# A transformer block on one core: the two small products of the forgetting-attention scores stacked in one contraction

## The chip, the cores and the metric

The kernel runs on one core of one Trainium2 chip. The metric is the device time of one execution in microseconds; the number quoted is the median of the runs. TensorE (PE) multiplies matrices, VectorE (DVE), ScalarE (ACT) and GpSimd (POOL) work on tiles of 128 partitions, SyncE (SP) and ACT start DMA transfers. Each engine runs its own list of instructions strictly in order, and waits on semaphores for the others.

## The reference, cut to what matters

Two transformer blocks over 1024 tokens of width 1024. The first block mixes pooling, gated linear attention and "Fox" attention with 8 heads of 64 channels, then an MLP; the second has multi-head latent attention ("MLA", 16 heads). Everything is float32. The change touches the Fox scores alone:

```
qh = heads(q) * (Dh ** -0.5)                       # 8 heads, Dh = 64
F  = cumsum(log_sigmoid(f_logit + b_f))
s  = einsum('bhqd,bhkd->bhqk', qb, kh) + Fb[..., None] - F[:, :, None, :]
s  = where(kpos <= qpos, s, -inf)
o  = softmax(s) @ v
```

## The kernel before, in words

**Precision.** A float32 operand is split in a "hi" part, rounded to the format that TensorE multiplies in one pass, and a "lo" part, the rest. A product is the sum of three: lo by hi, hi by lo, and hi by hi. This holds for the weight products (function `project`, line 220, 48 matmuls of 512 columns for a unit of 128 output channels) and for the scores.

**Fox buffers.** For each head there are four tiles of 128 partitions by 1024 tokens, each in two copies `b` = 0, 1 that alternate from head to head: `q_hi`, `q_lo`, `k_hi`, `k_lo`. Rows 0 to 63 hold the head's channels (line 967 by ACT; lines 983, 984, 987 by DVE). Row 64 of `k_hi` and `k_lo` holds the two parts of the forget sums, fetched by two row DMAs that ACT issues (line 963); row 65 of `q_hi` receives minus the row maximum by another row DMA (line 733). The constant rows are set once by POOL (line 1000). The contraction has 66 rows for scores and 65 for the row maxima.

**The step.** `steps` (line 843 and before) runs one step for each of the 8 heads: steps 0 and 1 written out, then a loop of two steps per turn. Step n projects the queries and keys of head n and finds its row maxima, and in the same step the scores, exponentials and value products of head n-1 are computed. TensorE's order in a step (`step_pe`, `attend_pe`):

- first half of the projection (24 matmuls), then scores 0 and 1 of head n-1, then the second half;
- twelve iterations g = 0 to 11 of `attend_pe`. The scores are cut in 12 pieces of at most 128 keys by 512 queries; their widths are 512, 384, 256, 256 (first half of the queries) and 512 five times, 384, 256, 256 (second half), six of 512, two of 384 and four of 256 in all. Iteration g has the value products of piece g (lines 622, 623: they wait for ACT's first exponential, line 668), the third value product of piece g-1 (line 629: waits for POOL, line 677), and the scores of piece g+2 (lines 606, 607, 608, and a mask matmul, 612, on the diagonal). After iterations 4 to 9 come the row maxima of head n (lines 652, 654, 655): maxima 0 and 1 after g = 4, 2 and 3 after g = 5, then one after each. Maxima 4 to 7 take PSUM banks again that DVE must have reduced: maximum 6 waits until maximum 4 is reduced;
- transposes of the values (638, 640), and of the eight maxima (660), which waits for DVE's line 717.

ACT computes two exponentials of each piece (668 to `p_hi`, 670 to `probs`), and between them what `fox_prepare_act` puts at certain g: the scaled copy of the queries at g = 1 (967), the copy of the values at g = 3 (973). After g = 6 it starts the softmax division of the first half (685, 687). POOL subtracts for each piece (677), then splits the weights of the next unit (1919, 1921). DVE splits queries and keys, reduces the maxima (712), and between maxima 3 and 4 does the division of the first half (698, 701, 707).

The last head has no step that projects another: `last_pe` and `last_act` attend to it alone.

## Time and profile before

| | |
|---|---|
| runs | 2280.11, 2282.21, 2282.62 us, median 2282.21 |
| profiled execution, span from first to last instruction | 2284.0 us |
| PE busy | 2128.9 us, 93% of the span |
| POOL, DVE, ACT busy | 1105.4, 1125.8, 671.8 us |
| mean granted TensorE clock | 0.964 of full speed |

The profiled execution has no time of its own beside its span, 2284.0 us, which lies 1.8 us above the median of the runs. The Fox stage is a small part: the steps of heads 1 to 7 run from 118.9 to 345.2 us of the span, the last head to 368.9 us. A row of the timeline gives the start and the length of an instruction (or of several alike that follow one another) and, in square brackets, how long the engine sat idle before it and what ended that. Matmuls overlap: the recorded length of one (0.40 us for 512 columns) is longer than the distance from its start to the next start, which is what it costs.

### The profile page before, as it was taken

What the parts mean: (1) busy time and instruction counts of PE and PEld (TensorE: products, weight loads), DVE (VectorE), ACT (ScalarE), POOL (GpSimd) and SP (SyncE); (2) the same over time, 40 slices, a digit from 0 to 9 for tenths busy, and PEclk for the clock granted to TensorE, in tenths of its full rate; (3) what the DMA queues carried; (4) which work ended last, traced back from release to release, by engine and by line L of the source; (5) the groups of instructions that cost most, each with busy time, mean ns of one, the idle gap of its engine ahead of it and who ended that gap; (6) DMA issues with size and microseconds to landing.
All of it is one profiled execution on the core that took longest, in us unless ns stands there. A gap on an engine that the chain in (4) does not pass through costs nothing.

```text
span 2284.0 us, 27160 instructions
## 1 busy us (share of the span) xinstructions
PE 2128.9 (93%) x9840; PEld 1691.4 (74%) x9840; DVE 1125.8 (49%) x1213; ACT 671.8 (29%) x1069; POOL 1105.4 (48%) x657
## 2 busy tenths in 40 slices
PE   5999999988999999999999998998999999989996
PEld 3777776877778878788878876886776777668774
DVE  6545653737541211212111287215777777754576
ACT  3334444221121000000001132114555555560322
POOL 1635554522833634633444383334656666653373
PEclk9999998997999999999999998998999999989998
DMA  3100000112211211211111131110000000001122
GB/s 139 48 19 20 14 14 19 46 38 92 92 46 53 67 55 46 74 46 54 57 55 46 55 101 37 46 46 28 20 19 19 19 19 19 19 28 46 46 69 97
DMA packets 31624, 106.98 MB, mean 47 GB/s; under 512 B 3440, under 2 KB 3632, under 8 KB 31568
## 3 DMA queue, kind: packets, MB, share of 16 engines
q1 hardware_dynamic: 27520, 96.53, 12.7%
q10 hardware_dynamic: 4048, 9.67, 1.2%
q8 instruction: 39, 0.64, 0.1%
q14 instruction: 17, 0.14, 0.0%
HBM read 101.83 MB, written 4.26 MB: 46 GB/s over the span
## 4 chain that ended last, share of the span: by engine, by line
PE 59%; POOL 15%; issue 14%; DVE 8%; ACT 2%; ACTq 0%; POOLq 0%; DMA 0%; DVEq 0%
PE ps L220 45%; POOL probs_lo L677 11%; PE ps L385 4%; PE ps L249 3%; PE ps L237 2%; POOL w_lo L1921 2%; POOL w_hi L1919 2%; DVE h_lo L366 1%; DVE tmp L1747 1%; DVE x L1749 1%; DVE S_all L1287 1%; DVE tmp L362 1%; DVE result L1753 0%; PE ps L1594 0%; DVE ssq L413 0%
## 5 line engine op out<-in xcount | busy, mean ns | idle before, releaser
L1919 POOL TENSOR_TENSOR w_hi<-w_raw,zero 128x1024 fp32r<-128x1024 f32 (+1 forms) x173 | 334.7, 1935 | 816.0 <-PE ps L220 575.7
L1921 POOL TENSOR_TENSOR w_lo<-w_raw,w_hi 128x1024 fp32r<-128x1024 f32 (+1 forms) x173 | 433.0, 2503 | 13.6
L220 PE MATMUL ps<-h_hi,w_lo 128*128 128x512 f32 x1328 | 338.4, 398 | 5.6 <-DVE x L512 5.1
L220 PE MATMUL ps<-h_hi,w_hi 128*128 128x512 f32 x1328 | 328.0, 389 | 0.0
L677 POOL TENSOR_TENSOR probs_lo<-probs,mla_p_hi 128x512 fp32r<-128x512 f32 x192 | 220.3, 1167 | 182.0 <-ACT probs L670 181.9
L220 PE MATMUL ps<-h_lo,w_hi 128*128 128x512 f32 x1216 | 302.0, 391 | 0.0
L220 PEld LDWEIGHTS ps<-h_hi,w_lo 128*128 128x128 f32 x1328 | 251.2, 191 | 61.6 <-issue 10.0
L220 PEld LDWEIGHTS ps<-h_hi,w_hi 128*128 128x128 f32 x1328 | 249.3, 188 | 51.7
L220 PEld LDWEIGHTS ps<-h_lo,w_hi 128*128 128x128 f32 x1216 | 230.0, 189 | 48.4
L1369 DVE TENSOR_TENSOR tmp<-ps,tmp 128x1024 f32<-128x1024 f32 x22 | 26.9, 1224 | 370.3 <-PE ps L220 363.6
L712 DVE TENSOR_REDUCE mx<-ps 128x1 f32<-128x256 f32 (+1 forms) x192 | 144.5, 785 | 78.5 <-PE ps L655 77.8
L677 POOL TENSOR_TENSOR probs_lo<-probs,fox_p_hi 128x512 fp32r<-128x512 f32 (+1 forms) x96 | 102.9, 1081 | 126.8 <-ACT probs L670 126.1
L670 ACT ACTIVATE probs<-ps 128x512 f32<-128x512 f32 (+2 forms) x288 | 145.7, 506 | 0.0
L512 DVE TENSOR_TENSOR x<-ps,x 128x1024 f32 x32 | 39.1, 1222 | 171.7 <-PE ps L220 165.1
L668 ACT ACTIVATE mla_p_hi<-ps 128x512 fp32r<-128x512 f32 x192 | 97.6, 508 | 85.2 <-PE ps L612 55.6
L1357 ACT ACTIVATE tmp<-ps 128x1024 f32<-128x1024 f32 x22 | 22.6, 1027 | 323.4 <-PE ps L220 323.3
L1359 ACT ACTIVATE a_hi<-tmp 128x1024 f32 x22 | 23.4, 1062 | 236.8 <-DVE tmp L1369 236.8
L622 PE MATMUL ps<-mla_p_hi,mla_vaug 128*128 128x512 f32 x192 | 79.4, 413 | 8.5 <-ACT mla_p_hi L668 6.8
L668 ACT ACTIVATE fox_p_hi<-ps 128x512 fp32r<-128x512 f32 (+1 forms) x96 | 48.5, 505 | 100.8 <-PE ps L612 94.3
L1371 DVE TENSOR_TENSOR a_lo<-tmp,a_hi 128x1024 f32 x22 | 59.8, 2718 | 29.4 <-ACT a_hi L1359 29.4
L629 PE MATMUL ps<-probs_lo,mla_vaug 128*128 128x512 f32 x192 | 68.7, 358 | 4.4 <-POOL probs_lo L677 4.4
L606 PE MATMUL ps<-mla_q_hi,mla_k_lo 97*128 97x512 f32 x192 | 69.1, 360 | 3.3 <-DMA mla_q_hi<-c_neg 3.3
(345 smaller groups left out, 3911.7 us busy)
## 6 DMA issues: line engine op xcount, KB each, us to landing
w_raw<-in_wpack SPq DMA_DIRECT2D x173, 512.0 KB, 3.3
x<-in_xT ACTq DMA_DIRECT2D x16, 512.0 KB, 8.3
out<-result SPq DMA_DIRECT2D x8, 512.0 KB, 2.9
p_raw<-in_pT ACTq DMA_DIRECT2D x1, 1024.0 KB, 7.2
const_stage<-in_consts SPq DMA_DIRECT2D x1, 788.0 KB, 4.4
pos_i<-in_pos SPq DMA_DIRECT2D x1, 512.0 KB, 6.4
vec<-in_vecs SPq DMA_DIRECT2D x1, 284.0 KB, 5.3
mla_q_hi<-c_neg ACTq DMA_DIRECT2D x16, 4.0 KB
```

What stands on the lines that cost most here:

```text
L220: last = nc.tensor.matmul(dst[:, half, :], w[slot][:, kt, :], a[:, i, t], start=(n == 0), stop=(n == total - 1))
L249: last = nc.tensor.matmul(dst[:, half, :], w[u % 2][:, kt, :], a[:, kt, cols(half)], start=(kt == 0 and n == 0), stop=(kt == DT - 1 and n ...
L385: last = nc.tensor.matmul(PS[:, bank, :], w[slot][:, kt, :], a[:, kt, t], start=(k == 0), stop=(k == 3 * len(order) - 1))
L606: nc.tensor.matmul(out, k_lo[b][r, keys], q_hi[b][r, t], start=True, stop=False)
L622: nc.tensor.matmul(PS[:, O_BANK[half], off:HALF], A.bufs[4][b][:, j, :], p, start=(j == 0), stop=False)
L629: nc.tensor.matmul(PS[:, O_BANK[half], off:HALF], A.bufs[4][b][:, j, :], P_lo[g % 4][:, 0:HALF - off], start=False, stop=(g in LAST_OF_HAL ...
L668: nc.scalar.activation(A.p_hi[g % 2][:, 0:HALF - off], scores, ACT.Exp).then_inc(A.p_hi_done, 1)
L670: nc.scalar.activation(Pt[g % 4][:, 0:HALF - off], scores, ACT.Exp).then_inc(A.exp_done, 1)
L677: nc.gpsimd.tensor_tensor(P_lo[g % 4][:, w], Pt[g % 4][:, w], A.p_hi[g % 2][:, w].bitcast(F32), ALU.subtract)\
L712: nc.vector.reduce_max(mx[:, i:i + 1], flat(PS[:, bank:bank + 2, :])[:, 0:max_width(i)[1]] if i >= 4 else PS[:, bank, 0:max_width(i)[1]], ...
L1919: nc.gpsimd.tensor_tensor(w_hi[s][:, kts, :], raw[s][:, kts, :], no_change[:, kts, :], ALU.add).then_inc(w_hi_done, 1)
L1921: nc.gpsimd.tensor_tensor(w_lo[s][:, kts, :], raw[s][:, kts, :], w_hi[s][:, kts, :].bitcast(F32), ALU.subtract)\
```

## The change

In the Fox attention `k_lo` and `q_lo` become stacks of 128 rows: `q_lo` holds the hi queries in rows 0 to 63 and the lo queries in rows 64 to 127, `k_lo` the lo keys in rows 0 to 63 and the hi keys in rows 64 to 127. One matmul over all 128 rows gives both small products. The hi by hi product still needs hi queries and hi keys on the same rows, so ACT copies both into `q_hi` and `k_hi` (two more copies of 64 by 1024). The two parts of the forget sums sit in rows 64 and 65 of `k_hi`, filled by one DMA of two rows; the row maximum moves to row 66. POOL sets 6 tiles at the start instead of 10. MLA keeps its three products.

```diff
-            nc.tensor.matmul(out, k_lo[b][r, keys], q_hi[b][r, t], start=True, stop=False)
-            nc.tensor.matmul(out, k_hi[b][r, keys], q_lo[b][r, t], start=False, stop=False)
+            if A is fox:
+                nc.tensor.matmul(out, k_lo[b][:, keys], q_lo[b][:, t], start=True, stop=False)
+            else:
+                nc.tensor.matmul(out, k_lo[b][r, keys], q_hi[b][r, t], start=True, stop=False)
+                nc.tensor.matmul(out, k_hi[b][r, keys], q_lo[b][r, t], start=False, stop=False)
             last = nc.tensor.matmul(out, k_hi[b][r, keys], q_hi[b][r, t], start=False, stop=not masked)
...
-        fox = Attention("fox", FOX_H, HD + 1, HD + 2, 0)
+        fox = Attention("fox", FOX_H, HD + 2, HD + 3, 0)
...
                     if A is fox:
-                        pe.wait_ge(A.f_in[b], turn * 32 + 32)
+                        pe.wait_ge(A.copied, (n + 1) * 2)
+                        pe.wait_ge(A.f_in[b], turn * 16 + 16)
...
-            for part, row in ((0, k_hi[b]), (1, k_lo[b])):
-                act.dma_start(row[HD:HD + 1, :].bitcast(F32), f_rows[part, bass.ds(n, 1), :]).then_inc(fox.f_in[b], 16)
+            act.dma_start(k_hi[b][HD:HD + 2, :].bitcast(F32), f_rows[:, bass.ds(n, 1), :].rearrange("a o t -> (a o) t")).then_inc(fox.f_in[b], 16)
...
-                nc.scalar.activation(q_hi[b][0:HD, :], src[0:HD, :], ACT.Copy, scale=HD ** -0.5).then_inc(fox.hi_done, 1)
+                nc.scalar.activation(q_lo[b][0:HD, :], src[0:HD, :], ACT.Copy, scale=HD ** -0.5).then_inc(fox.hi_done, 1)
+
+            def queries_again():
+                act.wait_ge(fox.hi_done, n * 2 + 1)
+                nc.scalar.activation(q_hi[b][0:HD, :], q_lo[b][0:HD, :].bitcast(F32), ACT.Copy).then_inc(fox.copied, 1)
+
+            def keys_again():
+                act.wait_ge(fox.hi_done, n * 2 + 2)
+                nc.scalar.activation(k_hi[b][0:HD, :], k_lo[b][HD:P, :].bitcast(F32), ACT.Copy).then_inc(fox.copied, 1)
...
-            return {1: queries, 3: values}
+            return {1: queries, 2: queries_again, 3: keys_again, 4: values}
...
-            nc.vector.tensor_copy(k_hi[b][0:HD, :], src[HD:P, :]).then_inc(fox.hi_done, 1)
-            nc.vector.scalar_tensor_tensor(q_lo[b][0:HD, :], src[0:HD, :], HD ** -0.5, q_hi[b][0:HD, :].bitcast(F32),
+            nc.vector.tensor_copy(k_lo[b][HD:P, :], src[HD:P, :]).then_inc(fox.hi_done, 1)
+            nc.vector.scalar_tensor_tensor(q_lo[b][HD:P, :], src[0:HD, :], HD ** -0.5, q_lo[b][0:HD, :].bitcast(F32),
                                            ALU.mult, ALU.subtract).then_inc(fox.lo_done, 1)
             dve.wait_ge(fox.hi_done, n * 2 + 2)
-            nc.vector.tensor_tensor(k_lo[b][0:HD, :], src[HD:P, :], k_hi[b][0:HD, :].bitcast(F32), ALU.subtract)\
+            nc.vector.tensor_tensor(k_lo[b][0:HD, :], src[HD:P, :], k_lo[b][HD:P, :].bitcast(F32), ALU.subtract)\
                 .then_inc(fox.lo_done, 1)
...
-                for dst, value in ((q_hi[b][HD:HD + 2, :], 1.0), (q_lo[b][HD:HD + 2, :], 0.0), (k_hi[b][HD:HD + 2, :], 1.0),
-                                   (k_lo[b][HD:HD + 2, :], 0.0), (vaug[b][:, :, HD:P], 1.0)):
-                    nc.gpsimd.memset(dst.bitcast(F32), value).then_inc(fox.setup, 1)
+                for dst in (q_hi[b][HD:HD + 3, :], k_hi[b][HD:HD + 3, :], vaug[b][:, :, HD:P]):
+                    nc.gpsimd.memset(dst.bitcast(F32), 1.0).then_inc(fox.setup, 1)
```

ACT's list in a step, from the scaled copy of the queries at g = 1 to the first exponential of piece 5; `fox_p_hi` and `probs` are written by the two exponentials of pieces 2, 3, 4 and 5 in turn. Before:

```order
L967 ACTIVATE fox_q_hi_92<-ps 64x1024
L668 ACTIVATE fox_p_hi_103<-ps 128x256
L670 ACTIVATE probs_81<-ps 128x256
L668 ACTIVATE fox_p_hi_104<-ps 128x256
L670 ACTIVATE probs_82<-ps 128x256
L973 ACTIVATE fox_vT<-mix 64x1024
L668 ACTIVATE fox_p_hi_103<-ps 128x512
L670 ACTIVATE probs_79<-ps 128x512
L668 ACTIVATE fox_p_hi_104<-ps 128x512
```

The same stretch of ACT's list in the changed kernel:

```order
L971 ACTIVATE fox_q_lo_94<-ps 64x1024
L671 ACTIVATE fox_p_hi_103<-ps 128x256
L673 ACTIVATE probs_81<-ps 128x256
L975 ACTIVATE fox_q_hi_92<-fox_q_lo_94 64x1024
L671 ACTIVATE fox_p_hi_104<-ps 128x256
L673 ACTIVATE probs_82<-ps 128x256
L979 ACTIVATE fox_k_hi_96<-fox_k_lo_98 64x1024
L671 ACTIVATE fox_p_hi_103<-ps 128x512
L673 ACTIVATE probs_79<-ps 128x512
L985 ACTIVATE fox_vT<-mix 64x1024
L671 ACTIVATE fox_p_hi_104<-ps 128x512
```

A copy stands ahead of the exponentials of piece 3, another ahead of those of piece 4, and the values' copy has moved from ahead of piece 4 to ahead of piece 5.

TensorE's list in iterations g = 3 and g = 4: value products, scores of pieces 5 and 6, and the first maximum. Before:

```order
L622 MATMUL ps<-fox_p_hi_104,fox_vaug_99 128x256
L623 MATMUL ps<-fox_p_hi_104,fox_v_lo_101 64x256
L629 MATMUL ps<-probs_lo_85,fox_vaug_99 128x256
L606 MATMUL ps<-fox_q_hi_91,fox_k_lo_97 128x512
L607 MATMUL ps<-fox_q_lo_93,fox_k_hi_95 128x512
L608 MATMUL ps<-fox_q_hi_91,fox_k_hi_95 128x512
L622 MATMUL ps<-fox_p_hi_103,fox_vaug_99 128x512
L623 MATMUL ps<-fox_p_hi_103,fox_v_lo_101 64x512
L629 MATMUL ps<-probs_lo_86,fox_vaug_99 128x256
L606 MATMUL ps<-fox_q_hi_91,fox_k_lo_97 128x512
L607 MATMUL ps<-fox_q_lo_93,fox_k_hi_95 128x512
L608 MATMUL ps<-fox_q_hi_91,fox_k_hi_95 128x512
```

The same two iterations in the changed kernel:

```order
L625 MATMUL ps<-fox_p_hi_104,fox_vaug_99 128x256
L626 MATMUL ps<-fox_p_hi_104,fox_v_lo_101 64x256
L632 MATMUL ps<-probs_lo_85,fox_vaug_99 128x256
L607 MATMUL ps<-fox_q_lo_93,fox_k_lo_97 128x512
L611 MATMUL ps<-fox_q_hi_91,fox_k_hi_95 128x512
L625 MATMUL ps<-fox_p_hi_103,fox_vaug_99 128x512
L626 MATMUL ps<-fox_p_hi_103,fox_v_lo_101 64x512
L632 MATMUL ps<-probs_lo_86,fox_vaug_99 128x256
L607 MATMUL ps<-fox_q_lo_93,fox_k_lo_97 128x512
L611 MATMUL ps<-fox_q_hi_91,fox_k_hi_95 128x512
```

One matmul of each piece's three score products is gone; nothing else has moved on this engine.

## Rows read from the trace of the kernel before

**Rows 1.** Stretches: us; busy of PE, PEld, DVE, ACT, POOL; PEclk; DMA share, GB/s.

```profile
148.00:156.00 8.00, 7.09 (x33) 5.39 (x32) 6.32 (x8) 1.72 (x4) 4.95 (x3) 0.79 0.14 42
181.00:190.00 9.00, 8.10 (x45) 6.44 (x44) 6.42 (x9) 1.88 (x4) 4.97 (x3) 1.00 0.16 61
151.50:184.60 33.10, 31.99 (x160) 24.55 (x159) 17.61 (x22) 14.82 (x30) 16.97 (x15) 0.95 0.05 17
1745.00:1755.00 10.00, 8.36 (x53) 6.25 (x53) 9.14 (x10) 4.69 (x11) 8.03 (x7) 1.00 0.00 0
```

**Rows 2.** Timeline (start, length in us), TensorE: scores 0, then projection.

```profile
158.70 0.40 PE L606 MATMUL ps<-fox_q_hi,fox_k_lo 66*128 66x512 f32 x1
158.93 0.40 PE L607 MATMUL ps<-fox_q_lo,fox_k_hi 66*128 66x512 f32 x1
...
162.02 1.98 PE L220 MATMUL ps<-h_lo,w_hi 128*128 128x512 f32 x8
```

**Rows 3.** Timeline, ACT: the same step, iterations 1 to 5.

```profile
165.84 1.02 ACT L967 ACTIVATE fox_q_hi<-ps 64x1024 fp32r<-64x1024 f32 x1 [4.33 <-PE ps L220]
...
166.76 0.37 ACT L668 ACTIVATE fox_p_hi<-ps 128x256 fp32r<-128x256 f32 x1
...
167.03 0.37 ACT L670 ACTIVATE probs<-ps 128x256 f32<-128x256 f32 x1
...
167.86 0.38 ACT L668 ACTIVATE fox_p_hi<-ps 128x256 fp32r<-128x256 f32 x1 [0.46 <-PE ps L612]
...
168.40 1.05 ACT L973 ACTIVATE fox_vT<-mix 64x1024 f32 x1
...
169.35 0.58 ACT L668 ACTIVATE fox_p_hi<-ps 128x512 fp32r<-128x512 f32 x1
...
170.30 0.59 ACT L668 ACTIVATE fox_p_hi<-ps 128x512 fp32r<-128x512 f32 x1
```

**Rows 4.** Timeline, TensorE: value products 3, 4, 5; mask and maximum 6.

```profile
168.76 0.28 PE L622 MATMUL ps<-fox_p_hi,fox_vaug 128*128 128x256 f32 x1
...
170.07 0.47 PE L622 MATMUL ps<-fox_p_hi,fox_vaug 128*128 128x512 f32 x1
...
171.84 0.48 PE L622 MATMUL ps<-fox_p_hi,fox_vaug 128*128 128x512 f32 x1
...
178.85 0.23 PE L612 MATMUL ps<-masks,ident_bf 128*128 128x128 bf16 x1
...
179.19 0.50 PE L652 MATMUL ps<-fox_k_hi,fox_q_hi 65*128 65x512 f32 x1
```

**Rows 5.** Timeline, DVE and POOL: division of the first half.

```profile
174.95 0.69 DVE L698 TENSOR_TENSOR newton<-ps,r 64x512 f32<-64x512 f32 x1
...
175.44 3.95 POOL L677 TENSOR_TENSOR probs_lo<-probs,fox_p_hi 128x512 fp32r<-128x512 f32 x3 [1.11 <-ACT probs L670]
...
175.68 1.60 DVE L701 SCALAR_TENSOR_TENSOR rec<-newton,r 64x512 f32<-64x512 f32 x1
...
177.46 0.68 DVE L707 SCALAR_TENSOR_TENSOR mix<-ps,rec 64x512 f32 x1 [0.18 <-DVE rec L701]
```

**Rows 6.** Timeline, end of the step: POOL, DVE, TensorE.

```profile
182.51 1.89 POOL L1919 TENSOR_TENSOR w_hi<-w_raw,zero 128x1024 fp32r<-128x1024 f32 x1
...
182.88 1.55 DVE L717 TENSOR_SCALAR mx<-mx 128x8 f32<-128x8 f32 x1
...
184.49 0.27 PE L660 MATMUL ps<-ident,mx 128*8 128x128 f32 x1 [0.69 <-DVE mx L717]
```

**Rows 7.** Timeline, TensorE: first score of the last head.

```profile
348.51 0.80 PE L606 MATMUL ps<-fox_q_hi,fox_k_lo 66*128 66x512 f32 x1 [3.28 <-DMA fox_q_hi<-c_neg]
```

**Rows 8.** Timeline, TensorE: a stall in the MLA stage.

```profile
1749.38 0.50 PE L652 MATMUL ps<-mla_k_hi,mla_q_hi 96*128 96x512 f32 x1 [0.74 <-DVE mx L712]
```

**Rows 9.** Timeline, step 0: ACT's queries, TensorE's first maximum.

```profile
103.27 1.02 ACT L967 ACTIVATE fox_q_hi<-ps 64x1024 fp32r<-64x1024 f32 x1 [12.85 <-POOL fox_vaug L1000]
...
108.33 0.28 PE L654 MATMUL ps<-fox_k_hi,fox_q_hi 65*128 65x256 f32 x1
```

More of the change, by code:

```diff
@@ L733, in max_row_act @@
             act.dma_start(A.bufs[0][b][A.rows - 1:A.rows, :].bitcast(F32), c_neg[:, :].bitcast(F32)).then_inc(A.row_in[b], 16)
-        fox = Attention("fox", FOX_H, HD + 1, HD + 2, 0)
+        fox = Attention("fox", FOX_H, HD + 2, HD + 3, 0)
         fox.bufs, fox.v_lo, fox.p_hi = buffers("fox", R_X, R_X + 24576, R_S + 8192, R_S + 20480, R_S + 24576)
         fox.f_in = [sem(f"fox_f_in{b}") for b in range(2)]
+        fox.copied = sem("fox_copied")
         fox_vT = at("fox_vT", R_S + 16384, [HD, T])
@@ L957, in fox_prepare_act @@
             if isinstance(n, int) and n == 0:
-                act.wait_ge(fox.setup, 10)
+                act.wait_ge(fox.setup, 6)
                 act.wait_ge(f_stored, 32)
@@ L980, in fox_prepare_dve @@
             if isinstance(n, int) and n == 0:
-                dve.wait_ge(fox.setup, 10)
+                dve.wait_ge(fox.setup, 6)
             dve.wait_ge(fox.hi_done, n * 2 + 1)
-            nc.vector.tensor_copy(k_hi[b][0:HD, :], src[HD:P, :]).then_inc(fox.hi_done, 1)
-            nc.vector.scalar_tensor_tensor(q_lo[b][0:HD, :], src[0:HD, :], HD ** -0.5, q_hi[b][0:HD, :].bitcast(F32),
+            nc.vector.tensor_copy(k_lo[b][HD:P, :], src[HD:P, :]).then_inc(fox.hi_done, 1)
+            nc.vector.scalar_tensor_tensor(q_lo[b][HD:P, :], src[0:HD, :], HD ** -0.5, q_lo[b][0:HD, :].bitcast(F32),
                                            ALU.mult, ALU.subtract).then_inc(fox.lo_done, 1)
             dve.wait_ge(fox.hi_done, n * 2 + 2)
-            nc.vector.tensor_tensor(k_lo[b][0:HD, :], src[HD:P, :], k_hi[b][0:HD, :].bitcast(F32), ALU.subtract)\
+            nc.vector.tensor_tensor(k_lo[b][0:HD, :], src[HD:P, :], k_lo[b][HD:P, :].bitcast(F32), ALU.subtract)\
                 .then_inc(fox.lo_done, 1)
```

## The prediction

> **What bounds the kernel.** I read the page first: TensorE is busy 93% of 2284.0 us, every other engine under half. So the time is TensorE's list plus its stalls, and I went to the Fox stage by stretches. In the step that starts at 151.5 us TensorE is busy 31.99 of 33.10 us, with a mean clock of 0.95 [rows 1]; POOL has 16.97 us and ACT 14.82. The timeline of TensorE shows what one score matmul costs: of 512 columns, 0.23 us from start to start, though each is recorded as 0.40 [rows 2]. By columns I take 0.17 for 384 and 0.12 for 256. Then the other engines' timelines, to see which waits are close behind: ACT in the first five iterations, where the change puts work [rows 3, 4], DVE and POOL in the division between the maxima [rows 5], and the step's end [rows 6].
>
> **What is removed.** One score matmul in each of 12 pieces: 6 x 0.23 + 2 x 0.17 + 4 x 0.12 = 2.2 us for a head. If TensorE alone set the pace, 8 heads would give 17.8 us. The stacked matmul has 128 rows where the old ones had 66; the hi by hi one grows to 67, the maxima to 66. I cost the rows at nothing: eight of the projection's 128-row matmuls take 1.98 us, the last one's tail of 0.4 included, which is the same 0.23 each [rows 2].
>
> **What is added, and where it stands.** ACT gets two copies of 64x1024 in each step. The nearest row is the values' copy, SBUF to SBUF in the same shape: recorded 1.05 us, next instruction 0.95 after its start [rows 3]. The bounds are the queries' copy from PSUM (0.92 to the next) and no overlap at all (1.05). ACT has 18 us spare in the step, but not here: in iterations 2 to 5 the pieces are narrow and TensorE is right behind ACT. I walk the step on the clock of before, with value product 0 held at its place (165.65 us, just ahead of rows 3).
>
> - Scores 0 and 1 lie inside the projection, where nobody but TensorE counts: 0.23 + 0.17 = 0.40 us earlier for all that follows. I add it at the end.
> - Exponential 2 stands at 166.76 as before, its second at 167.03, the queries' new copy at 167.30. It puts piece 3 at 168.25 instead of 167.86. Piece 3 is done at 168.63, so value product 3 starts at about 168.75, where it stood at 168.76 [rows 4]: the 0.47 us that scores 2, 3 and 4 gave are spent waiting.
> - Piece 3's second at 168.52, the keys' copy at 168.79, piece 4 at 169.74 instead of 169.35. Value product 4 starts 0.72 after its exponential did, so at 170.46: +0.4, after about 0.9 us of idle TensorE.
> - Piece 4's second at 170.22, the values' copy (moved) at 170.70, piece 5 at 171.65 instead of 170.30. Value product 5 at 172.38: +0.55. This is the worst point.
> - From here ACT is ahead again, and each iteration is shorter by its score matmul: value product 6 at +0.3, 7 at +0.1, 8 at -0.1.
> - Maximum 6 waited for DVE: 0.34 us from the mask's start, where these follow a mask after 0.04 [rows 4], so 0.30 of stall. DVE was late because its line 701, which reads two SBUF operands, took 1.60 us where its neighbours of the same shape take 0.69 and 0.68: POOL had begun piece 7 at 175.44, DVE came at 175.68, and the two take turns [rows 5]. In the changed kernel ACT reaches piece 7 late: its chain (exponentials 5 and 6, two division steps) is some 0.7 us behind, so POOL begins it near 176.1 to 176.2, while DVE, tied to TensorE's maximum 3 (+0.3), comes at 176.0. DVE is now first by about 0.1 to 0.2 us, line 701 takes 0.7, and the stall of 0.30 goes.
> - So value product 9 is at -0.5, and 10 at -0.6. The end keeps its shape: POOL's last piece, then its weight split of 1.89 us, behind which line 717 waits for 1.55, then TensorE's 0.69 us of idle before line 660 [rows 6]. All of it follows the last scores, so -0.6.
>
> The Trainium skill, "SBUF — State Buffer", section "SBUF: two separate sides", says that VectorE with two SBUF inputs and GpSimd share a port pair as an exclusive lock: whoever starts first holds it for the whole instruction. The stretched 701 agrees with that. By the rule order at one moment decides 0.9 us of DVE, so it is also what could turn the last 0.3 around (first rival).
>
> Per step: 0.40 + 0.60 = 1.0 us earlier, seven steps: 7.0 us.
>
> **The last head.** It starts after 3.28 us of idle on the row DMA [rows 7], without ACT copies. TensorE sets the pace for pieces 0 to 5 (0.23 + 0.17 + 0.12 + 0.12 + 0.23 + 0.23 = 1.1 us saved, up to 1.8 where the clock is at its lower level); behind that ACT and POOL do. I take 1.1.
>
> **Edits at nothing.** Four memsets fewer on POOL release ACT's first queries some 4 us earlier; they waited 12.85 us for POOL [rows 9], but TensorE projects values until 108.33 before it needs a maximum, and that cover stays. The single row DMA saves one issue in ACT's queue, during the projection, where ACT waits for TensorE (4.33 us even right before the queries' copy [rows 3]). The new wait of TensorE for both copies comes before maximum 0, after value product 4, which itself needs ACT to be past the second copy: never late. Maximum 2 needs the values' copy, done at 171.75, ahead of value product 5. DVE's three operations keep shapes and sources.
>
> **Sum.** 7.0 + 1.1 = 8.1 us off the profiled 2284.0: 2275.9. The median of the runs is 1.8 us under that execution, so 2274.2; I say 2274.5.
>
> **Rivals.**
>
> 1. *POOL keeps the lead over line 701.* For it: the margin of 0.1 to 0.2 us is no more than my errors along the walk. Then 701 ends with POOL's piece 7 plus 0.5 us, near 177.9 instead of 177.28, maximum 6 comes at 179.8, the end of the step at +0.45, less 0.40: nothing gained in seven steps, 1.1 in the last head. 2281.5. Some steps one way, some the other: between.
> 2. *The clock falls in the new idle (the other side).* In the step's end before the stretch 148 to 156 the granted clock was 0.79, in 181 to 190 1.00 [rows 1]: every second step end costs 0.21 x 8 = 1.7 us, after a little more idle than its neighbour. The change makes new idle ahead of value products 3, 4 and 5: 0.5 + 0.9 + 0.4 = 1.8 us in 4. Should TensorE drop to the lower of its two levels (1.2 instead of 2.4 GHz) there, a step costs 1.7 more instead of 1.0 less; from five steps of seven on the kernel is slower than before. All seven: 7 x 1.7 - 8.1 = +3.8, so 2286.0; with rival 1 on top 2293. Against it: in the MLA stage TensorE stalls 0.74 us between dense matmuls [rows 8] with the clock at 1.00 over that stretch [rows 1]. The Trainium skill, "TensorE: Matmul & The Clock Gate", section "What's actually happening", calls the throttled state the default, which activity releases; the row at 0.79 agrees, and nothing here has as much idle amid dense work as the new place.
> 3. *The falls that are there disappear.* The step ends keep their shape, but all stands elsewhere in time. There are three such falls (at the ends of 151, 216 and 281 us; those of 184, 249 and 314 have none, one of each kind in [rows 1]). All three gone: 5 us more, 2269.5. For it: ends so much alike, with and without a fall. Against it: the same every second end keeps its extra idle.
> 4. *The copies are covered and all 17.8 us come.* 2264.4. It needs a copy of under 0.5 us; the row says 0.95.
>
> With the copies at 1.05 the walk loses 0.2 us per step, with 0.92 it gains 0.06: 2276 to 2274.
>
> **Chances.** Forecast 0.53, own range 2272 to 2278; rival 1, or a mixture, 0.24; rival 2 0.09; rival 3 0.10; rival 4 0.04. The range leaves out rival 4, most of rival 2 and the far end of 3: 2269.5 to 2283. Below 0.2% (4.6 us; the runs lie 2.5 us apart) a measurement tells nothing. Faster by more: nearly all of the forecast, rivals 3 and 4, a little of the mixtures, 0.62. Slower by more: rival 2 in most steps with rival 1, and what I overlook, 0.08. Same 0.30.
>
> **What would show it.** Per step, from one line 660 to the next: about 1.0 us less. TensorE waits for ACT ahead of value products 3, 4 and 5 (0.5, 0.9, 0.4 us). Line 701's successor, shorter than 0.8 us in the first half of each step, and no stall ahead of maximum 6: right; 1.6 us or more: rival 1. Granted clock under 1 between value products 4 and 7: rival 2. Total TensorE work less by 96 matmuls. I am wrong on the first term if the step ends are not at least 0.4 us earlier, and on the copies if value product 5 doesn't come later, measured from value product 0, than before.

## The result and the profile after

The changed kernel takes 2270.82 us (median of 4 runs, 2268.62 to 2272.18), the kernel before 2282.41 us (4 runs, 2280.11 to 2283.28): a ratio of 0.9944, 95% interval 0.9927 to 0.9961. A second series gave 2272.00 us against 2282.63, ratio 0.9953 (0.9939 to 0.9967). The forecast was 2274.5, the range 2269.5 to 2283.0. So the kernel is faster, by 11.6 and 10.6 us where 8 were forecast. The forecast's own range began at 2272; the point is nearer to rival 3 (2269.5), which adds 5 us from the clock to the forecast's 8.

Between the two profiled executions the span falls by 13.6 us, from 2284.0 to 2270.4. The step ends split that up. In the changed kernel line 663 is what line 660 was; from one such row to the next:

| | first end | steps of heads 1 to 7 (us) | last end to first matmul behind Fox | from there to the end |
|---|---|---|---|---|
| before | 118.84 | 32.40, 33.25, 31.44, 33.46, 31.46, 33.42, 30.68 | 34.83 | 1904.2 |
| after | 117.79 | 31.58, 30.66, 30.44, 30.97, 30.42, 30.91, 29.66 | 33.08 | 1904.9 |
| difference | -1.05 | -0.82, -2.59, -1.00, -2.49, -1.04, -2.51, -1.02 | -1.75 | +0.7 |

The seven steps give 11.5 us. The other columns move with the execution as well: a second profile of each kernel has its first end at 118.28 before and 118.52 after, so the 1.05 us of that column are no gain of the change; its last head takes 36.24 before and 33.07 after; and its seven steps add up to 226.2 and 214.6 us, 11.7 apart. Steps 3, 5 and 7 have full clock in both kernels, and give the forecast's 1.0 us each. Steps 2, 4 and 6 give 2.5 us: before, each began with the clock at its lower level [rows 1], and now none does. The page of the changed kernel has 96 matmuls fewer (9744), and a mean granted clock of 0.969 where it was 0.964.

The stretches of the changed kernel that answer to [rows 1]: the first end of the three in question, the next end, and one whole step (columns as there):

```profile
148.17:154.37 6.20, 5.51 (x30) 4.44 (x29) 4.72 (x7) 0.97 (x2) 3.51 (x2) 1.00 0.20 61
...
178.83:185.03 6.20, 5.50 (x31) 4.52 (x30) 4.72 (x7) 0.97 (x2) 3.51 (x2) 1.00 0.25 78
...
149.37:180.03 30.66, 28.51 (x146) 21.34 (x146) 16.90 (x22) 16.60 (x32) 17.05 (x15) 1.00 0.06 19
```

TensorE now sits idle for 2.15 us of the 30.66 where it was idle for 1.11 of 33.10: the change has turned part of the work it removed into waiting. ACT has grown from 14.82 to 16.60 us.

TensorE's timeline, changed kernel, scores 0 and 1 inside the projection; they answer to [rows 2]:

```profile
155.15 0.39 PE L607 MATMUL ps<-fox_q_lo,fox_k_lo 128*128 128x512 f32 x1
...
155.38 0.39 PE L611 MATMUL ps<-fox_q_hi,fox_k_hi 67*128 67x512 f32 x1
...
155.65 0.42 PE L607 MATMUL ps<-fox_q_lo,fox_k_lo 128*128 128x384 f32 x1
```

128 rows cost what 66 did: 0.23 us from the first start to the second. Score 1 starts 0.50 after score 0, where the old lines 606 stood 0.74 apart (158.70 and 159.44).

ACT in iterations 1 to 5 (start, length; in brackets the idle time before), for [rows 3]:

```profile
161.87 1.02 ACT L971 ACTIVATE fox_q_lo<-ps 64x1024 fp32r<-64x1024 f32 x1 [4.14 <-PE ps L220]
162.79 0.36 ACT L671 ACTIVATE fox_p_hi<-ps 128x256 fp32r<-128x256 f32 x1
163.05 0.37 ACT L673 ACTIVATE probs<-ps 128x256 f32<-128x256 f32 x1
163.32 1.05 ACT L975 ACTIVATE fox_q_hi<-fox_q_lo 64x1024 fp32r<-64x1024 f32 x1
164.27 0.37 ACT L671 ACTIVATE fox_p_hi<-ps 128x256 fp32r<-128x256 f32 x1
164.53 0.37 ACT L673 ACTIVATE probs<-ps 128x256 f32<-128x256 f32 x1
164.93 1.06 ACT L979 ACTIVATE fox_k_hi<-fox_k_lo 64x1024 fp32r<-64x1024 f32 x1
165.89 0.57 ACT L671 ACTIVATE fox_p_hi<-ps 128x512 fp32r<-128x512 f32 x1
166.37 0.58 ACT L673 ACTIVATE probs<-ps 128x512 f32<-128x512 f32 x1
166.97 1.06 ACT L985 ACTIVATE fox_vT<-mix 64x1024 f32 x1
167.94 0.57 ACT L671 ACTIVATE fox_p_hi<-ps 128x512 fp32r<-128x512 f32 x1
```

No row after the first has an idle time: ACT runs without a gap from 161.87, and is the engine that TensorE waits for. A copy takes 0.95 us to the next start, as the forecast took it.

TensorE in the same step, for [rows 4]: value products 3, 4 and 5, then the mask and maximum 6.

```profile
164.69 0.39 PE L625 MATMUL ps<-fox_p_hi,fox_vaug 128*128 128x256 f32 x1 [0.20 <-ACT fox_p_hi L671]
...
166.61 0.47 PE L625 MATMUL ps<-fox_p_hi,fox_vaug 128*128 128x512 f32 x1 [0.84 <-ACT fox_p_hi L671]
...
168.56 0.50 PE L625 MATMUL ps<-fox_p_hi,fox_vaug 128*128 128x512 f32 x1 [0.21 <-ACT fox_p_hi L671]
...
174.84 0.23 PE L615 MATMUL ps<-masks,ident_bf 128*128 128x128 bf16 x1
174.88 0.47 PE L655 MATMUL ps<-fox_k_hi,fox_q_hi 66*128 66x512 f32 x1
```

The three waits are where the forecast put them. Maximum 6 follows its mask after 0.04: its stall is gone.

DVE and POOL in the division, for [rows 5]:

```profile
172.19 0.69 DVE L704 SCALAR_TENSOR_TENSOR rec<-newton,r 64x512 f32<-64x512 f32 x1
...
172.43 4.49 POOL L680 TENSOR_TENSOR probs_lo<-probs,fox_p_hi 128x512 fp32r<-128x512 f32 x4 [0.82 <-ACT probs L673]
```

DVE's line 704 (the old 701) starts 0.24 us ahead of POOL's piece 7, and takes 0.69 instead of 1.60 us.

The step's end, for [rows 6], keeps its shape:

```profile
178.06 1.89 POOL L1930 TENSOR_TENSOR w_hi<-w_raw,zero 128x1024 fp32r<-128x1024 f32 x1
...
178.43 1.55 DVE L720 TENSOR_SCALAR mx<-mx 128x8 f32<-128x8 f32 x1
...
180.03 0.27 PE L663 MATMUL ps<-ident,mx 128*8 128x128 f32 x1 [0.70 <-DVE mx L720]
```

The first score of the last head, for [rows 7], still waits 3.28 us for the row DMA, 12.5 us earlier; and step 0, for [rows 9], shows ACT's queries 4.6 us earlier with TensorE's first maximum only 0.33 earlier:

```profile
98.63 1.02 ACT L971 ACTIVATE fox_q_lo<-ps 64x1024 fp32r<-64x1024 f32 x1 [8.53 <-POOL fox_vaug L1011]
...
108.00 0.28 PE L657 MATMUL ps<-fox_k_hi,fox_q_hi 66*128 66x256 f32 x1
...
335.99 0.80 PE L607 MATMUL ps<-fox_q_lo,fox_k_lo 128*128 128x512 f32 x1 [3.28 <-DMA fox_q_hi<-c_neg]
```

### The profile page after: what moved, and what is told of

Same layout as the page of the kernel before. It is cut to its first block, busy times and chain, and to the rows that moved or that the text cites. A ratio compares the mean times of both kernels' runs of the same rounds, so it can differ in the third digit from the quotient of the medians.

```text
span 2270.4 us, 26966 instructions
## 1 busy us (share of the span) xinstructions
PE 2106.5 (93%) x9744; PEld 1669.2 (74%) x9744; DVE 1118.9 (49%) x1213; ACT 685.6 (30%) x1085; POOL 1101.0 (48%) x653
## 4 chain that ended last, share of the span: by engine, by line
PE 58%; POOL 15%; issue 15%; DVE 9%; ACT 2%; ACTq 0%; POOLq 0%; DMA 0%; DVEq 0%
PE ps L220 45%; POOL probs_lo L680 11%; PE ps L385 4%; POOL w_lo L1932 2%; PE ps L237 2%; PE ps L249 2%; POOL w_hi L1930 2%; DVE h_lo L366 1%; DVE tmp L1758 1%; DVE x L1760 1%; DVE S_all L1298 1%; DVE tmp L362 1%; DVE ssq L1846 0%; DVE result L1764 0%; PE ps L1605 0%
## 5 line engine op out<-in xcount | busy, mean ns | idle before, releaser
L1932 POOL TENSOR_TENSOR w_lo<-w_raw,w_hi 128x1024 fp32r<-128x1024 f32 (+1 forms) x173 | 432.5, 2500 | 13.6
```

What stands on the lines that cost most here:

```text
L1932: nc.gpsimd.tensor_tensor(w_lo[s][:, kts, :], raw[s][:, kts, :], w_hi[s][:, kts, :].bitcast(F32), ALU.subtract)\
```

## The experiments

All were compared with the kernel before on the same chip. In the quoted expectations theory A is the account of the prediction: removed matmuls at their price, copies that hold TensorE up, the shared port, and falls of the clock apart from all that. What the other letters stand for is told in the texts themselves. The totals turned out a poor gauge for a single step: from the first matmul behind Fox to the end the same code takes 1898.6 to 1904.9 us from one profile to another, while the steps of the same kernel agree within 0.08 us (the first of them apart). So most verdicts below rest on the step lengths, and this table has them. A star marks a step, from the second on, that begins with a fall of the clock at the end before it (the first begins at the lower level in all of them).

| kernel | steps of heads 1 to 7 (us) |
|---|---|
| no_copies | 31.96, 31.10*, 31.15*, 29.83, 29.55, 29.79, 28.79 |
| copies_three_products | 32.74, 33.53*, 31.70, 33.64*, 32.09, 32.20, 31.34 |
| division_no_lock | 33.27, 31.25, 31.31, 33.11*, 31.29, 33.11*, 30.52 |
| values_first | 32.29, 31.64*, 30.00, 30.40, 31.58*, 30.38, 29.24 |
| keys_late_dve_copy | 31.25, 30.61, 30.23, 30.93, 30.24, 30.91, 29.47 |
| queries_early_keys_late | 30.61, 29.79, 29.67, 31.71*, 29.67, 31.66*, 30.45* |
| after_later | 32.16, 30.68, 30.44, 30.96, 30.43, 30.94, 29.67 |
| before_later_10 | 32.35, 33.19*, 31.43, 33.47*, 31.46, 33.46*, 30.69 |
| values_first_later | 31.15, 30.12, 30.00, 31.83*, 30.00, 30.38, 30.82* |

### no_copies: the matmul gone, without the copies

The kernel before, without one small product in Fox:

```diff
-            nc.tensor.matmul(out, k_hi[b][r, keys], q_lo[b][r, t], start=False, stop=False)
+            if A is not fox:
+                nc.tensor.matmul(out, k_hi[b][r, keys], q_lo[b][r, t], start=False, stop=False)
```

> The kernel before without the product of the hi keys with the lo queries (line 607) in all 12 Fox pieces of a head: TensorE's list as short as in the changed kernel, no second copies, the values' copy where it was. That product is left out of the scores. Theory A (my walk: the matmuls are worth 2.2 us a head, and ACT's copies eat the part of it between value products 2 and 5): steps of heads 1 to 7 shorter by 2.0 us each (0.40 in the projection, 1.6 behind it) against 1.0 in the changed kernel; no stall of 0.8 us ahead of value product 4; 2282.4 - 14 - 1.5 = 2267 with the three clock falls at the step ends still there, 2262 with them gone. Theory B (POOL and ACT would pace the step anyway, the copies cost little): steps shorter by no more than 1.2 us, 2270 to 2273.

Measured: 2262.83 us (4 runs), ratio 0.9909 (0.9892 to 0.9925). Steps 5 and 7, at full clock in both, are 1.91 and 1.89 us shorter than before. The removed matmul is worth 1.9 us of the 2.2 it costs, and against the changed kernel (0.87 less in steps 5 and 7, 1.14 and 1.12 in 4 and 6) the copies cost about 1.0 us in each step, as A has it. TensorE's waits between 118 and 335 us (us in total, times, longest), here and, in the second fence, in the changed kernel; line 623 here is 625 there, the value product:

```profile
PE ps L623 <- ACT fox_p_hi L669: 4.3, 7, 0.7
```

```profile
PE ps L625 <- ACT fox_p_hi L671: 8.0, 18, 0.8
```

Even without the new copies TensorE waits 4.3 us for ACT, once in each step, where it waited 0.7 us before the change: the shorter list of TensorE runs into the values' copy, which was there all along. That is 0.6 us a step. Part of it comes back at maximum 6: here too DVE reaches the line that was 701 ahead of POOL's piece 7 (172.72 against 172.94 us in step 2), and it takes 0.68 or 0.69 us in all seven steps. So the 1.9 us are the 2.2, less a new wait, plus an old stall that is gone; these parts add up to 1.7 or 1.8 in steps 5 and 7, and the rest was not followed. The new copies double the total of the waits.

### copies_three_products: the copies without the saving

The changed kernel, with the stacked matmul issued twice:

```diff
                 nc.tensor.matmul(out, k_lo[b][:, keys], q_lo[b][:, t], start=True, stop=False)
+                nc.tensor.matmul(out, k_lo[b][:, keys], q_lo[b][:, t], start=False, stop=False)
```

> The changed kernel with the stacked matmul issued twice (the small products are counted twice): ACT's list as in the changed kernel, TensorE's as long as before. Theory A: the copies alone cost: value product 4 at +0.4 and 5 at +0.6 us from value product 0, little of it made up, steps 0.3 to 0.4 us longer than before where neither has a clock fall, so +2.5 us: 2285 with falls, 2280 if they go. Theory B: copies are covered, steps as long as before within 0.1 us.

Measured: 2281.75 us (10 runs), ratio 0.9992 (0.9980 to 1.0004). All steps but the sixth are 0.18 to 0.66 us longer than before (steps 3, 5 and 7: 0.26, 0.63, 0.66), which is A's mechanism. The total isn't longer, and my number for it (2285) was a miss: step 6 lost its fall, and nothing in this run says why.

Steps 3 and 5 have the same instructions and full clock, and differ by 0.39 us (31.70 and 32.09). The trace shows where. The line that was 701 is 705 here; POOL's row is piece 7. In step 3, then in step 5:

```profile
207.08 0.68 DVE L705 SCALAR_TENSOR_TENSOR rec<-newton,r 64x512 f32<-64x512 f32 x1
207.08 1.83 POOL L681 TENSOR_TENSOR probs_lo<-probs,fox_p_hi 128x512 fp32r<-128x512 f32 x1 [0.81 <-ACT probs L674]
...
272.40 1.29 POOL L681 TENSOR_TENSOR probs_lo<-probs,fox_p_hi 128x512 fp32r<-128x512 f32 x1 [0.81 <-ACT probs L674]
272.41 1.82 DVE L705 SCALAR_TENSOR_TENSOR rec<-newton,r 64x512 f32<-64x512 f32 x1
...
276.00 0.50 PE L656 MATMUL ps<-fox_k_hi,fox_q_hi 66*128 66x512 f32 x1 [0.20 <-DVE mx L716]
```

The two reach their instructions within 0.01 us of each other. Where POOL is ahead, it takes its usual 1.29 us and DVE 1.82; where it is not, DVE takes 0.68 and POOL 1.83. In step 5 maximum 6 starts 0.43 us behind its mask (275.57), in step 3 0.04 behind (210.25 and 210.29): the same 0.39. Step 7 is like step 5, steps 1, 2, 3, 4 and 6 like step 3. This is rival 1, in two steps of seven and in the one kernel where the race is this close. It also says what the copies cost by themselves: 0.63 and 0.66 us against a kernel before whose 701 is just as long (steps 5 and 7), and 0.39 against `division_no_lock` below, where it is just as short (step 3). Beside the shorter list of TensorE the same copies cost 0.87 to 1.14 us a step: the halves of the change don't add, since a shorter list exposes more of the copies.

### division_no_lock: DVE's division without a second SBUF operand

The kernel before; in Fox, line 701 reads its second operand from PSUM:

```diff
-            nc.vector.scalar_tensor_tensor(rec[rows, :], newton[0:HD, :], -2.0, r0[0:HD, :], ALU.add, ALU.mult).then_inc(A.newton, 1)
+            second = PS[HD:P, O_BANK[half], :] if A is fox else r0[0:HD, :]
+            nc.vector.scalar_tensor_tensor(rec[rows, :], newton[0:HD, :], -2.0, second, ALU.add, ALU.mult).then_inc(A.newton, 1)
```

> The kernel before, with the second operand of line 701 taken from PSUM and not from SBUF in Fox (a wrong factor in the division). Theory A (the stall of 0.3 us ahead of maximum 6 comes from line 701 taking turns with POOL): line 701 takes 0.7 us and not 1.6, the stall goes, steps shorter by 0.3 us, 2282.4 - 2 = 2280.3. Theory B (the stall comes from the length of DVE's list, the port doesn't matter): 701 stays at 1.6 or the stall stays, no change.

Measured: 2280.58 us (10 runs), ratio 0.9990 (0.9979 to 1.0001); steps 3 to 7 are 0.13, 0.35, 0.17, 0.31 and 0.16 us shorter. DVE's division and TensorE's mask and maximum 6 in the step that starts at 151.30:

```profile
174.06 0.69 DVE L702 SCALAR_TENSOR_TENSOR rec<-newton,ps 64x512 f32<-64x512 f32 x1
```

```profile
177.22 0.23 PE L612 MATMUL ps<-masks,ident_bf 128*128 128x128 bf16 x1
177.26 0.48 PE L652 MATMUL ps<-fox_k_hi,fox_q_hi 65*128 65x512 f32 x1
```

0.69 us instead of 1.60, and no stall ahead of maximum 6. The link from the long 701 to the stall is shown. It is worth 0.31 and 0.35 us in steps 4 and 6, as the forecast had it, and 0.13 to 0.17 in steps 3, 5 and 7. That is because the forecast read the stall in an even step. In step 3 of the kernel before, maximum 6 starts 0.17 us behind its mask (210.45 and 210.62), a stall of 0.13.

### values_first: the copies away from the narrow pieces

The changed kernel, with the values' copy ahead of all and the two new ones behind pieces 3 and 4:

```diff
-            return {1: queries, 2: queries_again, 3: keys_again, 4: values}
+            if isinstance(n, int) and n == 0:
+                return {1: queries, 2: queries_again, 3: keys_again, 4: values}
+            return {0: values, 1: queries, 3: queries_again, 4: keys_again}
```

> The changed kernel with ACT's copies in another order from step 1 on: the values' copy ahead of the exponentials of piece 1, while ACT waits for the projection, then queries after piece 1, the second queries after piece 3, the second keys after piece 4. Theory A (what is left of the cost is where the copies stand): value products 3 and 4 no longer wait for a copy, 5 at about its old distance, steps shorter than in the changed kernel by 0.5 to 0.7 us, 2270.8 - 4.5 = 2266.3 without new clock falls. Theory B (the copies' place doesn't matter, since TensorE's wait moves to DVE or POOL): 2270 to 2272.

Measured: 2268.82 us (6 runs), ratio 0.9941 (0.9927 to 0.9954). The steps without a fall (3, 4, 6, 7) are 0.44, 0.57, 0.53 and 0.42 us shorter than the changed kernel's, two of them under the 0.5 to 0.7 that I gave. TensorE's waits between 118 and 335 us:

```profile
PE ps L625 <- ACT fox_p_hi L671: 4.3, 7, 0.7
...
PE ps L657 <- ACT fox_k_hi L979: 1.1, 3, 0.4
```

The waits for the exponentials fall from 8.0 to 4.3 us, and a little comes back at maximum 0, which needs the keys' copy. The total gains less than the steps: this kernel has two falls where the changed one has none.

### after_again, before_again, before_later: is a fall luck?

The changed kernel and the kernel before once more, and the kernel before with five matmuls more ahead of its Fox stage, whose result is overwritten; they were meant to move the stage by 1.1 us:

```diff
             pe.wait_ge(w_split, U_FV[1] + 3)
+            for _ in range(5):
+                nc.tensor.matmul(FV_BANKS[1][:, 0, :], w_hi[U_FV[1] % 2][:, 0, :], h_hi[:, 0, 0:HALF], start=True, stop=True)
             project(pe, U_FV[1] % 2, range(DT), h_hi, h_lo, FV_BANKS[1])
```

> The changed kernel once more, unchanged, for a second profile and a longer series. Theory C (the three clock falls at the ends of every second step, which were in the first profile of before and not in the first of after, come and go with where the step ends stand in time, from execution to execution, and are not removed by the change): the steps without a fall are again 30.4 to 31.0 us long, some ends may show a fall of 1.4 to 1.7 us now, and the median lies 2 to 4 us above the first series or the same, 2270 to 2275. Theory D (the change itself removes them, since TensorE's work about the step's end is different): no fall at any step end again.

> The kernel before once more, for a second profile. Theory C: another pattern of falls at the step ends is possible, and odd steps without one are 31.4 us again. Theory D: the same three ends (about 151, 216, 281 us) show a fall again.

> The kernel before with five more matmuls of 512 columns (1.1 us) in the values' projection ahead of the Fox steps (overwritten by the projection, so nothing else changes): all step ends later by 1.1 us. Theory C: the number of ends with a fall may differ from three; steps without a fall keep their length. Theory D: three falls as in before.

Measured: the changed kernel 2272.00 us (5 runs), its steps 31.49, 30.66, 30.41, 30.99, 30.41, 30.94, 29.68, no fall at the end of any step from 1 to 6. The kernel before, 2282.73 (one run): steps 32.55, 33.18, 31.46, 33.48, 31.45, 33.42, 30.70, falls at the step ends of 150.83, 215.47 and 280.40 us, which are those of steps 1, 3 and 5 again. With five matmuls more, 2283.23 (one run): falls at the same three ends, 151.30, 215.94 and 280.85. But its first end stands at 118.79 us, and at 118.84 and 118.28 in the two profiles without them: the five matmuls did not move the stage as they were meant to, and this run is one more profile of the kernel before. What the three show is that C in its first form is out: the falls aren't drawn anew in each profiled execution. They came at the same step ends although the whole stage stood up to 0.56 us apart.

### keys_late_dve_copy: one copy to DVE

Values first, the keys' copy at iteration 4, and the queries' second copy on DVE behind its three operations:

```diff
-            return {1: queries, 2: queries_again, 3: keys_again, 4: values}
+            if isinstance(n, int) and n == 0:
+                return {1: queries, 3: keys_again, 4: values}
+            return {0: values, 1: queries, 4: keys_again}
...
                 .then_inc(fox.lo_done, 1)
+            nc.vector.tensor_copy(q_hi[b][0:HD, :], q_lo[b][0:HD, :].bitcast(F32)).then_inc(fox.copied, 1)
```

> The version that the runs so far point to: values' copy first as in values_first, the second copy of the queries on DVE behind its three operations, the second copy of the keys on ACT after piece 4. Theory A: value products 3 and 4 wait for no copy and 5 hardly, what is left is a stall of some 0.5 us ahead of maximum 0, which needs both copies; steps shorter than in values_first by 0.2 to 0.5 us, 2268.8 - 2.5 = 2266.3. Theory B: DVE's copy (two sides in SBUF) collides with POOL and the maxima come later by as much: 2268 to 2270.

Measured: 2273.34 us (6 runs), ratio 0.9961 (0.9948 to 0.9974), 7 us over what I expected and 3 over theory B's 2270. The six runs lie far apart, 2264.9 to 2278.7, and the profile is of the fastest, so the steps speak for that one alone. Steps 2 to 7 are only 0.00 to 0.21 us shorter than the changed kernel's. TensorE's waits, 118 to 335 us:

```profile
PE ps L657 <- DVE fox_k_lo L997: 4.3, 4, 1.1
...
PE ps L657 <- DVE fox_q_hi L999: 3.6, 3, 1.2
```

DVE's end of its three operations, its copy, and TensorE's maximum 0 in one of these steps:

```profile
256.71 1.23 DVE L997 TENSOR_TENSOR fox_k_lo<-ps,fox_k_lo 64x1024 fp32r<-64x1024 f32 x1
257.97 0.82 DVE L999 CAST fox_q_hi<-fox_q_lo 64x1024 fp32r<-64x1024 f32 x1
```

```profile
258.89 0.36 PE L657 MATMUL ps<-fox_k_hi,fox_q_hi 66*128 66x256 f32 x1 [1.07 <-DVE fox_k_lo L997]
```

The wait for ACT is gone whole, and one of 1.1 us ahead of maximum 0 stands in its place: DVE is done with the copy at 258.79, TensorE starts at 258.89. (The trace names line 997, done at 257.94; it is the copy that came last.) I had counted DVE's free time in the step, and not when its result is due. Of theory B a part is there too: POOL begins piece 7 some 0.8 us ahead of line 704, which takes 1.00 to 1.07 us in all seven steps instead of 0.68.

### after_later, before_later_10, values_first_later: does the place in time decide?

Ten such matmuls ahead of the Fox stage, in the changed kernel, in the kernel before, and in values_first:

```diff
+            for _ in range(10):
+                nc.tensor.matmul(FV_BANKS[1][:, 0, :], w_hi[U_FV[1] % 2][:, 0, :], h_hi[:, 0, 0:HALF], start=True, stop=True)
```

> The changed kernel with ten more matmuls of 512 columns (2.3 us) ahead of the Fox steps, overwritten by the values' projection; the steps themselves are the same. The falls at step ends are the same in every profile of a kernel so far (three in three profiles of before, none in two of after), but stood at other ends in values_first and no_copies. Theory C2 (a fall comes where a step end happens to stand in time, and the standing is the same in each execution): with the ends 2.3 us later at least one shows a fall, its step 1.5 us longer; steps without one 30.4 to 31.0 us. Theory D (the change's own mix of work at the end removes them): still none.

> The kernel before with the same ten matmuls ahead. Theory C2: fewer than three falls, or at other ends than those of steps 1, 3 and 5. Theory D: three falls at the same ends.

> values_first with the same ten matmuls ahead (2.3 us of added work). Theory C2: its two falls (ends of steps 1 and 4) go or move; if both go, 2268.8 + 2.3 - 3 = 2268; if they stay 2271. Theory D: falls at the same two ends.

The first end moved by 2.3 to 3.3 us in the first two (120.78 us from 117.79 and 118.52, and 121.61 from 118.84 and 118.28), and by 2.2 in the third (119.85 from 117.70).

Measured: 2273.07 us (one run) for the changed kernel, no fall at the end of any step from 1 to 6, so what C2 expected of it was wrong. 2288.48 us (one run) for the kernel before, with falls at 153.96, 218.58 and 283.51: the ends of the same three steps. 2270.25 us (4 runs) for values_first, ratio 0.9946 (0.9925 to 0.9966): here the falls are at other ends, those of steps 3 and 6 and not of 1 and 4. Stretches from 1.2 us ahead of a step's end to 5 us behind it (columns as in [rows 1]). In the kernel before, the ends of steps 1 and 2:

```profile
150.04:156.24 6.20, 5.50 (x23) 4.18 (x22) 4.69 (x7) 0.97 (x2) 3.48 (x2) 0.72 0.22 68
183.29:189.49 6.20, 5.51 (x31) 4.52 (x30) 4.72 (x7) 0.96 (x2) 3.51 (x2) 1.00 0.22 80
```

In values_first, the ends of steps 1, 3 and 4:

```profile
148.79:154.99 6.20, 5.51 (x23) 4.35 (x23) 4.70 (x7) 0.97 (x2) 3.49 (x2) 0.72 0.25 78
...
210.43:216.63 6.20, 5.29 (x29) 4.20 (x28) 4.72 (x7) 0.97 (x2) 3.51 (x2) 1.00 0.24 65
240.83:247.03 6.20, 5.51 (x24) 4.38 (x23) 4.69 (x7) 0.96 (x2) 3.48 (x2) 0.72 0.22 83
```

In values_first_later, the same three:

```profile
149.80:156.00 6.20, 5.50 (x30) 4.44 (x29) 4.72 (x7) 0.97 (x2) 3.51 (x2) 1.00 0.18 64
...
209.92:216.12 6.20, 5.28 (x23) 4.05 (x22) 4.69 (x7) 0.96 (x2) 3.48 (x2) 0.72 0.22 73
241.75:247.95 6.20, 5.50 (x31) 4.50 (x30) 4.73 (x7) 0.97 (x2) 3.52 (x2) 1.00 0.25 81
```

The busy times of such a stretch are the same in all of these with and without a fall (5.50 and 5.51, or 5.28 and 5.29 where TensorE also waits 0.2 us at the turn of the loop). With the fall TensorE gets through 23 or 24 matmuls, without it 29 to 31. TensorE's busy and idle time around the end doesn't decide, then. That the place in time does is a reading of one pair of profiles: values_first has no second profile, and the ends of the two versions don't differ by one shift (149.99 and 151.00 us for step 1, 211.63 and 211.12 for step 3), since a fall itself moves all that follows.

The fall isn't an answer to the wait at once either. Here is its stretch in the first profile of the kernel before, and the same 3.4 us behind the step's end in the changed kernel:

```profile
152.00:155.40 3.40, 3.40 (x10) 2.63 (x9) 2.76 (x5) 0.00 (x0) 1.60 (x1) 0.50 0.17 48
...
150.13:153.53 3.40, 3.40 (x16) 2.82 (x15) 2.80 (x5) 0.00 (x0) 1.63 (x1) 1.00 0.13 31
```

The wait of 0.69 us ends at 151.24 with the clock at 1.00, and the clock falls to half only 0.8 us later, amid dense matmuls. Over all profiles it falls between 0 and 1.3 us behind a step's end.

The two versions of values_first also price a fall, since each has steps with one where the other has none: 31.64 and 30.12, 31.83 and 30.40, 31.58 and 30.00, 30.82 and 29.24, so 1.4 to 1.6 us.

### queries_early_keys_late: the best placing

From values_first, the queries' second copy one piece earlier:

```diff
-            return {0: values, 1: queries, 3: queries_again, 4: keys_again}
+            return {0: values, 1: queries, 2: queries_again, 4: keys_again}
```

> values_first with the second copy of the queries after piece 2 and not 3; the keys' stays after piece 4. Theory A (my walk): value product 3 waits for the copy as in the changed kernel, 4 and 5 for none, steps shorter than in values_first by 0.3 us where neither has a fall, 2266 to 2268. Theory B (what bounds the stretch is the wait of maximum 0 for the keys' copy, which stays): no change in the steps, 2268 to 2270.

Measured: 2267.66 us (6 runs), ratio 0.9940 (0.9923 to 0.9957). TensorE's waits, 118 to 335 us:

```profile
PE ps L625 <- ACT fox_p_hi L671: 2.0, 7, 0.3
...
PE ps L657 <- ACT fox_k_hi L979: 1.1, 3, 0.4
```

The waits for the exponentials are down to 0.3 us a step, and its steps without a fall (29.79, 29.67, 29.67) are 0.75 to 0.87 us shorter than the changed kernel's, and step 3 is 0.33 under that of values_first, as theory A gave; step 5 is 0.12 us over the one without any copies. So nearly all of what the copies cost (0.87 us in step 5) is a matter of their place in ACT's list, as A says. Three falls take most of that back in the total. By its steps this is the best version; by its total its interval overlaps that of the changed kernel.

## Why the prediction was right, and where not

The mechanism of the steps is right, and its sum too: 6.6 us against 7.0. The total came out 3.7 us under the forecast because the three clock falls went as well. The forecast had them stay and gave their going (rival 3) a chance of 0.10; nothing in its reasoning about matmuls and copies says that they go.

**Right: the price of a score matmul and of its rows.** 0.23 us from start to start with 128 rows. Between the step's end and value product 0 steps at full clock are 0.42 us shorter (12.60 us from 184.49 to 197.09 before, 12.18 from 180.03 to 192.21 after); 0.40 was forecast.

**Right: the walk, with its small terms off.** Measured from value product 0, in the step that begins at 151.24 before and 149.37 after:

| | forecast | measured |
|---|---|---|
| value product 3 | 0.0 | -0.09 |
| 4 | +0.4 | +0.52 |
| 5 | +0.55 | +0.70 |
| 6, 7, 8 | +0.3, +0.1, -0.1 | +0.49, +0.29, +0.08 |
| 9, 10 | -0.5, -0.6 | -0.36, -0.47 |
| step's end | -0.6 | -0.48 |

The keys' copy starts 0.40 us after the exponential ahead of it, where 0.27 was forecast; that 0.13 runs through the rest of the list. In the next step the end is at -0.58. There the parts are not quite those of the forecast: the stall of maximum 6 that goes was 0.13 us and not 0.30, and the step gained 1.0 us all the same; what makes up for it was not followed. Back in the step of the table, the recorded idle ahead of products 3, 4 and 5 is 0.20, 0.84 and 0.21, together 1.25 us, where 1.8 was forecast. That sum understates the loss: scores 2 to 6 gave 0.93 us, product 5 still comes 0.70 later, so 1.63 us are gone. I take the rest for waits of the weight loads, which have rows of their own for the same releaser; no run isolated that.

**Right: line 701.** Its successor takes 0.69 us here, and 0.68 or 0.69 in all seven steps where 701 took 1.58 to 1.66. DVE was first by 0.24 us, forecast 0.1 to 0.2. So rival 1 is out for this kernel, and `division_no_lock` showed what hangs on it: 0.3 us in the steps that the forecast read, about half of that in the others. It was out by little: in `copies_three_products` a lead of POOL of 0.01 us brought it back in two steps of seven. The forecast's "the two take turns" isn't what the rows show: the one that starts first takes its usual time (POOL 1.29 us, DVE 0.69), and only the other is stretched (DVE to 1.60, and here POOL to 1.59). The rule of the Trainium skill, "SBUF — State Buffer", section "SBUF: two separate sides", that the one that starts first holds the port pair for its whole instruction, agrees with both orders of the race.

**Right: the clock in the new idle.** TensorE sits idle 0.84 us ahead of value product 4, and the granted clock stays at 1.00 over the whole step. Rival 2 is out. The copies at 0.95 us rule out rival 4.

**Mis-sized or not, it can't be told: the last head.** 1.75 us against 1.1 taken, inside the "up to 1.8 where the clock is at its lower level". But in the second pair of profiles it is 3.17 us (36.24 and 33.07). The mean clock over the stretch is 0.85 and 0.81 in the two profiles of the kernel before, 0.90 in both of the changed kernel. So the difference holds a part that is the clock's, and how much the removed matmuls give is open.

**Wrong: "the same every second end keeps its extra idle".** That was my argument against rival 3, and it gave that rival 0.10. The extra idle is indeed still there (at 210.97 and 272.33 us TensorE waits 0.23 and 0.20 us at the loop's turn), but no fall comes with it. Nor did it go with every fall before: it stands at 216.41 and 281.31 us (0.21 and 0.20), and at 151 us, where the first of the three falls is, there is none ([rows 1] has 0.91 us of idle in 8 there, and 0.90 in 9 at the end of 184). Rival 3 happened, on top of the forecast. Its price can be read at one place: from the step's end to the first score, 7.46 us with the fall (151.24 to 158.70) and 5.78 without (149.37 to 155.15), so 1.68; at the next such ends 7.67 and 6.06, and 7.64 and 6.02, so 1.61 and 1.62. Three falls make 4.9 us, and rival 3 said 5. What is left of the seven steps' 11.5 is 6.6, where the forecast said 7.0.

**Slips of the forecast's arithmetic.** In rival 2 a step with a new fall is said to cost "1.7 more instead of 1.0 less"; its total of +3.8 has 1.7 on top of the 1.0 gained, so 0.7 more a step. And 2275.9 less 1.8 is 2274.1, not 2274.2. Neither changes the forecast.

**The sum.** 6.6 for the steps, 4.9 for three falls, 1.75 for the last head, 1.05 ahead of the first end, and 0.7 lost behind Fox: 13.6 us between the two profiles. The last three belong to this pair: in the second (13.8 us between the spans) the last head gives 3.17, the first end comes 0.24 later, and 0.8 is lost behind Fox, beside 11.66 for steps and falls. Only the steps and the falls repeat. The medians differ by 2 us less: a span lies 1.8 us under the time of its execution (2270.4 and 2272.18), so the profile of before was of an execution some 3.4 us over its median, the one after 1.4 over.

**Open.** What picks the ends at which the clock falls. Shown: it is the same in each profile of a kernel that has more than one (the ends of steps 1, 3 and 5 in four profiles of the kernel before, one of them with its stage 3 us later; none in three of the changed kernel, one of them later by 2 to 3 us); it isn't TensorE's busy or idle time around the end; and two versions with the same steps, 2 us apart at the start, have it at different ends. That leaves how the ends stand in time: in the kernel before the falls come at step ends 64.6 to 64.9 us apart, in the others 31 to 92. No run sets these lengths by themselves, so that is argued only. The Trainium skill, "TensorE: Matmul & The Clock Gate", section "HAM oscillation — how this bites in real kernels", describes a clock that falls again at each long wait for a DMA; here no DMA is waited for at these ends, and the clock falls at some of several with the same 0.69 us wait and the same busy time, which that picture doesn't sort. So the 4.9 us from the falls are measured, and why this change removes them is not known.

## What to carry to other kernels

A removed matmul is worth its full price only up to the next engine in line: look for where TensorE already follows closely behind another engine, and put added work of that engine elsewhere in its list (here some 0.8 us a step of 0.9 to 1.1 came back by moving two copies). For a step that repeats, compare the lengths of steps and not totals: they agreed within 0.08 us from profile to profile (the first step apart), where the time of the same code behind them moved by 6 us. Where a stage has regular falls of the clock, count them apart from the change's own gain, since every version here that changed the steps' lengths had another set of them than the kernel before, or none, at 1.4 to 1.7 us each here. And where two engines come to the same place within 0.1 us, look at every repeat of the step: one of them may have gone the other way.
